# Packing 16 experts into ten blocks of 128 slots instead of eleven, with one more weight buffer

## What is computed

```python
sel = sigmoid(t @ w_router) + router_bias          # 384 tokens, 16 experts in 4 groups
best = argmax(sum of the two largest sel in each group)
idx = top_k(sel inside the best group, 2)          # two experts for each token
gates = one_hot(idx) * scores / sum
hid = silu(t @ w_gate[e]) * (t @ w_up[e])          # 1024 -> 256, for each expert e
out = sum_e (hid * gate_e) @ w_down[e]             # 256 -> 1024
```

## Time and profile before

| | |
|---|---|
| profiled execution | 799.34 us, its span 797.6 us |
| TensorE busy | 742.6 us, 93% |
| VectorE, ACT, POOL busy | 329.5, 216.4, 142.0 us |
| mean granted TensorE clock | 0.989 |
| HBM read and written | 202.02 and 13.93 MB, 271 GB/s over the span |
| layer 0: first gate/up to last down | 262.97 to 396.4 us |
| layer 1: the same | 637.80 to 771.6 us |

### The profile page before, as it was taken

How to read it: one execution, slowest core, us unless ns; L and a number is a source line. 1 busy time by engine, 2 the same in 40 slices (tenths; PEclk the granted TensorE clock), 3 DMA queues, 4 the chain that set the end, 5 groups by cost and what they waited for, 6 DMA issues and landing times. The chain is left out here.

```text
span 797.6 us, 9586 instructions
## 1 busy us (share of the span) xinstructions
PE 742.6 (93%) x3528; PEld 372.2 (47%) x3528; DVE 329.5 (41%) x874; ACT 216.4 (27%) x492; POOL 142.0 (18%) x238
## 2 busy tenths in 40 slices
PE   3999997999999999999999999889999799999994
PEld 1456652455446444443344755345545544444331
DVE  2023534656436453212272262564643734331136
ACT  2210255724023110111312025683312301101121
POOL 4146041120011200000212404222000120000202
PEclk9999998999999999999999999999999999999998
DMA  8997225679422999999897233657420499999961
GB/s 323 387 341 252 95 107 211 219 283 400 181 74 114 390 392 409 424 424 422 315 389 246 83 106 112 212 176 295 190 106 1 158 409 357 418 424 421 424 241 79
DMA packets 66340, 211.56 MB, mean 265 GB/s; under 512 B 7883, under 2 KB 8755, under 8 KB 54003
## 3 DMA queue, kind: packets, MB, share of 16 engines
q1 hardware_dynamic: 52744, 179.33, 58.1%
q10 hardware_dynamic: 7851, 17.70, 5.8%
q0 software_dynamic: 5696, 13.89, 4.9%
HBM read 202.02 MB, written 13.93 MB: 271 GB/s over the span
## 5 line engine op out<-in xcount | busy, mean ns | idle before, releaser
L2228 PE MATMUL bank<-ring,work 128*64 128x512 f32 (+1 forms) x512 | 157.6, 598 | 3.0 <-DMA ring<-in_w_up_dram 2.5
L2228 PEld LDWEIGHTS bank<-ring,work 128*64 128x64 f32 (+1 forms) x512 | 59.1, 158 | 96.0 <-issue 94.4
L2244 PE MATMUL bank<-ring,xs_tok 128*64 128x512 f32 (+1 forms) x256 | 79.9, 597 | 2.0 <-DVE xs_tok L1573 1.0
L1573 DVE COPY xs_tok<-bank 128x256 f32<-128x256 f32 x22 | 9.3, 424 | 149.2 <-PE bank L2235 149.2
L1858 PE MATMUL bank<-hT,ring 128*128 128x384 f32 x192 | 62.2, 486 | 0.0
L1732 PE MATMUL bank<-ring,cpad 128*32 128x512 f32 x384 | 49.4, 636 | 6.6 <-DMA ring<-in_w_ada_dram 5.8
L1858 PEld LDWEIGHTS bank<-hT,ring 128*128 128x128 f32 x192 | 36.5, 190 | 25.0
L2244 PEld LDWEIGHTS bank<-ring,xs_tok 128*64 128x64 f32 (+1 forms) x256 | 28.3, 157 | 39.1 <-issue 35.0
L990 ACT ACTIVATE xs_tok<-bank 128x256 f32<-128x256 f32 x22 | 8.5, 385 | 139.7 <-PE bank L2228 139.7
L2116 PE MATMUL bank<-ring,xn 128*128 128x512 f32 x96 | 43.6, 597 | 0.0
L997 ACT ACTIVATE qkv<-bank 128x512 f32<-128x512 f32 x40 | 21.7, 595 | 79.4 <-PE bank L2244 79.4
(11 more groups left out here) (392 smaller groups left out, 1057.2 us busy)
## 6 DMA issues: line engine op xcount, KB each, us to landing
ring<-in_w_ada_dram SPq DMA_DIRECT2D x48, 1024.0 KB, 8.8
ring<-in_w_gate_dram SPq DMA_DIRECT2D x32, 1024.0 KB, 13.1
ring<-in_w_up_dram SPq DMA_DIRECT2D x32, 1024.0 KB, 16.8
ring<-in_w_down_dram SPq DMA_DIRECT2D x32, 1024.0 KB, 14.6
ring<-in_w_in_dram SPq DMA_DIRECT2D x16, 1024.0 KB, 14.5
ring<-in_w_out_dram SPq DMA_DIRECT2D x8, 1024.0 KB, 7.3
y_exp<-qkv ACTq DMA_DIRECT2D x16, 512.0 KB, 8.4
xpad<-gate_rows ACTq DMA_DIRECT2D x6, 512.0 KB, 4.9
```

The lines of the kernel that those rows point to most:

```text
L1573: dve.tensor_copy(hidT[:, b, :], bank[2][:, 0:F]).then_inc(s_htc, 1)
L2228: last = mm(bank[b][i * n:(i + 1) * n, :].rearrange("p (i f) -> p i f", i=2), rows_T[:, kt * P + i * n:kt * P + (i + 1) * n], gate_up_of(s ...
L2244: last = mm(bank[5 + hf][i * n:(i + 1) * n, :], hidT[:, b, f * P + i * n:f * P + (i + 1) * n], w[:, f, hf * 512:(hf + 1) * 512], start=f = ...
```

## The change

`FIXED` goes from 2 to 3, each fixed expert gets 96 slots, the ranked ones 128 (two), 96 (two), 64 (eight) and 32 (the last). These sum to 1280, ten blocks with no slot left: 0 to 5 hold experts in parts of 32, 64 or 128 slots (an expert may lie in two blocks), 6 to 9 pairs of 64. Blocks 0, 2 and 5 have four parts of 32 columns, each with its own products; block 1 has two of 64. The down unit of pair 1 is loaded in two halves, expert 2's before the ranking. Ahead of it now are experts 0, 1, 2, the down unit of pair 0 and that half. A seventh buffer, `extra`, lies over the normed tiles and padding that the expert stage leaves free, and holds a unit from when the token rows are stored until block 7 at the latest. Each load counts on one of seven semaphores. With the new blocks the planner finds a free slot after nearly every block. `LISTS` becomes 0, 1, 2 to 5, 6 to 9; the list of block 1, which now has expert 2's tokens, is made behind the ranking on VectorE, and on TensorE behind all fillers. A block's result is stored in one or two pieces (twelve in all for seven stored blocks). VectorE's first weighting moves behind the loop.

```diff
-FIXED = 2
+FIXED = 3
-SLOTS = 6
+SLOTS, EXTRA, LANDED = 6, 6, 7
...
-PAIRS = ("fixed", "light", "heavy", "light", "heavy", "light", "light", "light")
...
+FULL, WIDE, NARROW = 2, 4, 12
+FIXED_CAP = 96
+RANK_OF = [None if _x < FIXED else _r for _x, _r in zip(range(E), (0, 0, 0, 2, 0, 1, 3, 12, *range(4, 12)))]
+cap_of = lambda r: CAP if r < FULL else HALF + CAP // 4 if r < WIDE else HALF if r < NARROW else CAP // 4
...
+BLOCKS = [parts_of(*quarters(0, 0, 1, 2), *quarters(1, 0)),
+          parts_of((1, Q, HALF), (2, 0, HALF)),
+          parts_of(*quarters(2, 2), *quarters(3, 0, 1, 2)),
+          parts_of((4, 0, CAP)),
+          parts_of((5, 0, CAP)),
+          parts_of(*quarters(6, 0, 1, 2), *quarters(7, 0))] + [parts_of((x, 0, HALF), (x + 1, 0, HALF)) for x in (8, 10, 12, 14)]
...
+SPLIT = (1, 2)
+MOE_UNITS = [(0, 0), (0, 1), (1, 0), (0, 2), SPLIT]
...
+EXTRA_LAST = STORED
...
+    if in_extra(_u):
+        _holder[EXTRA] = max(_last, default=None)
+    _s = min(_holder, key=lambda s: -1 if _holder[s] is None else RELEASED[_holder[s]])
...
-        xn = sb("xn", NT, DM)
+        arena = sb("arena", NT * DM + XM * 512)
+        xn = arena[:, 0:NT * DM].rearrange("p (t c) -> p t c", t=NT)
...
+        extra = arena[:, DM:DM + UNIT]
...
-        LISTS = ((0, 1), (1, 2), (2, 7), (7, NB))
-        ROWS_AT = 5
+        LISTS = ((0, 1), (1, 2), (2, 6), (6, NB))
+        ROWS_AT = 4
...
+                    if (pair, k) == (SPLIT[0], 1):
                         sp.wait_ge(s_order, l + 1)
...
+                    if EARLIER[u] is not None:
+                        sp.wait_ge(*used(EARLIER[u]))
+                    else:
+                        sp.wait_ge(s_h, 16 * NT * (l + 1))
+                        sp.wait_ge(s_x1, 2 * NT * (l + 1))
...
+                    for x, lo, n, at in stores_of(e):
+                        dma(y_exp[row_at(x) + lo:row_at(x) + lo + n, :], y_buf(e)[at:at + n, :]).then_inc(y_stored[b], 16)
...
-                fixed_one_hot(0)
-                fixed_one_hot(1)
+                one_hots(*LISTS[0])
...
                 slot_tokens(0)
                 step(dve.tensor_reduce(rank.unsqueeze(2), perm_tmp, AX.X, ALU.add))
-                slot_tokens(1)
...
                 dve.tensor_scalar(order, R(4)[:, 16 + FIXED:16 + E], -1.0, float(E), ALU.mult, ALU.add
                                   ).then_inc(s_order, 1)
+                one_hots(*LISTS[1])
                 step(dve.tensor_tensor(by_rank, rt[:, 1, :, FIXED:E].unsqueeze(2).broadcast_to([P, NT, RANKED, RANKED]),
                                        perm.unsqueeze(1).broadcast_to([P, NT, RANKED, RANKED]), ALU.mult))
+                slot_tokens(1)
                 step(dve.tensor_reduce(ranked_pos.unsqueeze(3), by_rank, AX.X, ALU.add))
...
+                    narrow = count_key[:, FIXED:E]
+                    step(dve.tensor_scalar(narrow, rank, float(NARROW), float(Q), ALU.is_gt, ALU.mult))
+                    step(dve.tensor_tensor(cap_row[:, FIXED:E], cap_row[:, FIXED:E], narrow, ALU.subtract))
...
-                    if e == NB - 2:
-                        weighted(0)
+                weighted(0)
                 weighted(1)
...
                 pe.wait_ge(s_btc, 6 * l + 2)
                 clock_kept(4, 2)
                 lists(0)
-                lists(1)
-                clock_kept(4, 4)
+                clock_kept(4, 6)
                 if l == 0:
                     ada_columns(ADA_GAP)
-                clock_kept(4, 4)
+                clock_kept(4, 2)
+                lists(1)
...
-                        for i, s in enumerate(slots):
-                            last = mm(bank[b][i * n:(i + 1) * n, :].rearrange("p (i f) -> p i f", i=2),
-                                      rows_T[:, kt * P + i * n:kt * P + (i + 1) * n], gate_up_of(s)[:, kt, :, :],
+                        for s, at, n in parts:
+                            last = mm(bank[b][at:at + n, :].rearrange("p (i f) -> p i f", i=2),
+                                      rows_T[:, kt * P + at:kt * P + at + n], gate_up_of(s)[:, kt, :, :],
                                       start=kt == 0, stop=kt == KT - 1)
```

More of the change, by code:

```diff
@@ L110, with in_extra @@
 SLOT, EARLIER = [], []
+EXTRA_LAST = STORED
+def in_extra(u):
+    for at in MOE_AT:
+        if at + SLOTS <= u < at + MOE_U:
+            p, k = MOE_UNITS[u - at]
+            return (GU_BLOCK[2 * p + k] <= EXTRA_LAST) if k < 2 else DN_BLOCK[p] < EXTRA_LAST
+    return False
 for _u in range(len(ORDER)):
@@ L469, in columns @@
                     sp.wait_ge(*used(EARLIER[u]))
-                load(u % SLOTS, [(slot(u)[:, 4 * i:4 * i + 4, :], v[:, 4 * i:4 * i + 4, :]) for i in range(2)])
+                load(u % LANDED, [(slot(u)[:, 4 * i:4 * i + 4, :], v[:, 4 * i:4 * i + 4, :]) for i in range(2)])
             def ada_unit(u, n):
@@ L572, in _ @@
             pool.iota(iota[:, CAP + 6:CAP + 6 + E], pattern=[[CAP, E]], base=-1, channel_multiplier=0)
-            at = {r: b * CAP + HALF * i for b, (p, part) in enumerate(BLOCKS) if RANK_AT[p]
-                  for i, r in enumerate(RANK_AT[p][k] for k in part)}
-            for r in range(0, RANKED, 2):
-                pool.iota(iota[:, 192 + r:194 + r], pattern=[[at[r + 1] - at[r], 2]], base=at[r] - 1, channel_multiplier=0)
+            at = ROW_AT[FIXED:]
+            r = 0
+            while r < RANKED:
+                run = next((i for i in range(2, RANKED - r) if at[r + i] - at[r + i - 1] != at[r + 1] - at[r]), RANKED - r)
+                pool.iota(iota[:, 192 + r:192 + r + run], pattern=[[at[r + 1] - at[r] if run > 1 else 0, run]],
+                          base=at[r] - 1, channel_multiplier=0)
+                r += run
             pool.iota(iota[:, 160:160 + E], pattern=[[-1, E]], base=E, channel_multiplier=0).then_inc(s_iota, 1)
@@ L2220, in rows_transposed, with gate_up @@
                     last.then_inc(done, 1)
-                def gate_up(b, rows_T, slots, done, between=None):
-                    n = P // len(slots)
+                def gate_up(b, rows_T, parts, done, between=None):
                     for kt in range(KT):
```

210 lines of the change are left out of this document (119 added, 91 removed).

## The result

The changed kernel takes 796.3 us (median of 20 runs, 787.86 to 799.63), the kernel before 799.92 us (20 runs, 797.27 to 803.07): the ratio is 0.9947, with a 95% interval of 0.9931 to 0.9964. That is 3.6 us faster, and 1.8 us more than the predicted 794.5. The profiled execution is one of the longer ones: 798.94 us, span 797.2, against 799.34 and 797.6 before. A second profile of the same kernel, taken for the experiments, has a span of 794.2.

The account below looks back on a forecast made before the run. The expert stages were taken as balanced, TensorE and the weight stream finishing together, with the stream setting the time from G2 on. Layer 0's -1.0 and layer 1's -3.8 gave -4.8 us: 799.34 to 794.5, range 784 to 802.

Parts of the forecast that it names:

- G2: The end of gate/up of block 2 in a layer's expert stage: 291.2 us in layer 0, 666.8 in layer 1 before.
- (1) Ten blocks: TensorE loses one period, 11.7 us per layer, if nothing else binds; a four-part block costs the same within 0.2 us.
- (2) Earlier units and an earlier order: Before the ranking: 4.5 units instead of 3 are in, and the order of experts is ready about 1 us sooner.
- (3) The stream after G2: Fifteen units stream from G2 on; the last down starts at G2 + 97.0, 4.4 us sooner per layer.
- A clock dip there: At the last gate/up: waiting lowers TensorE's clock, costing 1.0 us, covered by the last down's weights coming 1.1 us later.
- (4) The shift of G2: Block 1's list moved, so its gather gets TensorE on 3.9 us later in layer 0, 1.7 in layer 1.
- no wait before block 1: Sign of a wrong forecast: TensorE not waiting for block 1's rows, where a gap of 3 to 4 us was expected.
- The sentence on the wait for the stored rows: SP's wait for stored rows before the seventh buffer's load is over before it, the first gather being issued at 257.03.
- (5) What is free: Twelve stores on ACT's queue cost nothing; 0.9 us more VectorE work before block 1's hidden product fits its 1.4 us slack.
- (6) The tail: After the last down, results come a block earlier: about 1.1 us saved in layer 1, 0.5 in layer 0.
- The forecast's own case: In both expert stages a late gather shifts G2 and the stream pays: 794.5 us, range 791 to 797, chance 0.43.
- The first rival: Block 1's gather is not late, its list moved into time that costs nothing, G2 stays: 789 us, chance 0.20.

Follow-up runs that it names:

- the run in which both last downs waited for their own weights: Changed kernel with SP's ranked loads waiting for block 0's gathered rows, plus ten fillers before the last gate/up: 789.06 us, ratio 0.9829 to the kernel before.
- the kernel with the repair: Changed kernel, with SP waiting before the first ranked expert's load until block 0's rows are gathered: 786.69 us, ratio 0.9831 to the kernel before.
- twenty fillers: Changed kernel with twenty useless filler products on TensorE before the wait for the last gate/up's weights: 799.95 us, ratio 0.9994 to the kernel before.

## Why the prediction was right, and where it was not

**What bounds the kernel** was right: the weight stream from G2 on. Half a unit less is worth 2.6 us a layer, a unit more behind G2 costs 3.7 (7.5 over two layers), and 4.6 us of added TensorE work a layer cost 1.7, each with an error of 1.5 us a layer.

**(1) Ten blocks.** A four-part gate/up takes 7.05 us, one in two parts 7.09: "the same within 0.2 us" holds. The block taken off did not pay by its 11.7 us; 5 us of it stand as waiting before the last gate/up. The Trainium skill says that a change of tiling mode drains TensorE (TensorEngine Tiling (Array Packing), Key Properties). The trace does not contradict it, but shows no price: from gate/up to gate/up a four-part block takes 11.8 us (291.29 to 303.09 in layer 0), where a period was 11.7 before.

**(2) Earlier units and an earlier order.** The facts were right (1.1 us sooner, 258.05). What they do to the row stores and to the first gather was left out. With the early units ahead of them the row stores of layer 0 landed in a median of 5.4 us (4.4 in the second trace, 2.8 before), and the gather's issue moved from 257.03 to 258.58 or 257.55; the earlier order put the ranked loads ahead of it or 0.6 us behind. So the earlier order was a loss. The early units by themselves are a gain: held back as well, they cost 4.6 us a layer.

**(3) The stream after G2.** G2 + 97.0 was predicted, 96.0 and 97.3 were measured, and 95.2 and 97.0 in the run in which both last downs waited for their own weights. The last gate/up was put at + 83 and came at + 81.4 and + 82.1. The wait before it was put at 8 us and is 5: TensorE comes there at G2 + 76.5 and + 76.9, not + 74.9, and the weights 1 to 1.5 us sooner. A clock dip there was booked at 1.0 us and its cover at 1.1; the dips are 1.7 and 2.4 us, and only in layer 1 of the second trace does the last down still wait for its weights (0.56 us).

**(4) The shift of G2** is the step that failed. It said "all of it shifts G2" of the gather of block 1, +3.9 and +1.7, and took the gather of block 0 as unchanged. In layer 0 the gather of block 0 was late, by 5.2 us (9.2 us from issue to rows, where the kernel before has 4.0) and 1.55 us in its issue, with part of the first transposes and products at the granted 0.50; block 1 then came for nothing, which is one of the prediction's own signs of being wrong ("no wait before block 1"). Together +7.1 (second trace +5.8). In layer 1, where the first gather is 1.4 us ahead of the loads and lands in 4.4 us, it was block 1 as predicted, with 9.95 us of latency (10.3 taken), but with a dip of the clock behind it: +3.2 against 1.7. The sentence on the wait for the stored rows was where it could have been seen: it said that this wait was over before the loads, because the gather used to be issued at 257.03, and did not ask what the added loads do to those stores.
From issue to rows the gathers took 4.0 us with nearly empty queues and 8.5 to 10 beside weight loads. The Trainium skill's fit is 2.0 us plus bytes at 436 GB/s (DMA: Bandwidth & Descriptors, Anatomy of one DMA); for the 70 rows of 4 KB of block 0 that is an estimate of 2.7, short of both.

**(5) What is free** was: neither the stores nor the combination shows as a wait; block 1's hidden product is never waited for. **(6) The tail** is 1.6 us shorter in layer 1, predicted 1.1; layer 0's, predicted 0.5, is not there (+0.2).

**The sum** of -4.8 stands against -3.6 in the medians, and -0.4 and -3.4 in the two traces. Against the first trace G2 was taken 3.2 us too early in layer 0 and 1.5 in layer 1, the stretch behind it 1.1 too long and 0.5 too short, the tails 0.7 too short (layer 0) and 0.5 too long: together 4.3 of the 4.4 us by which that trace is above the sum, the rest is rounding. Against the second it is 1.4, since both stretches behind G2 are 5.3 us shorter there where 4.4 was taken. So the median lies near the forecast because the stream paid somewhat more than its booked 4.4, and the gathers cost 8.5 to 10.3 us where 5.6 were booked. That these two errors have opposite signs is luck: the sum is closer than its terms. The forecast's own case, a gather shifts G2 and the stream pays, is the one that happened, in layer 0 with another gather. The first rival, "the gather is not late", is the kernel with the repair: 786.7, where it said 789.

## What to carry to other kernels

A small transfer that many wait for has to be issued well ahead of large ones (here 1.4 us was enough each time, 1.3 once of two times, 0.6 never), and work that is moved "out of the way" can let the large ones start first: look at which queue gets its order sooner, not only at what the moved step itself delays. Where the engine that waits also releases the next loads, holding the loads back for it can fill the queues better. In the kernel before, whose gather had its lead already, the same wait cost 0.3%. A block taken off an engine pays only what the other resource allows, so ask first what shortens the stream, here the seventh buffer (7.5 us, against a net 3.6 for the whole change).

## What was not expected of the hardware

How much a lead of a microsecond goes with. Gather of block 0, layer 0, from its issue to the transposes of its rows:

| kernel | first ranked load after the gather's issue, us | issue to rows, us |
|---|---|---|
| changed, first trace | -0.53 | 9.2 |
| without the seventh buffer | +0.56 | 8.5 |
| changed, second trace | +0.57 | 8.6 |
| twenty fillers | +1.27 | 7.2 |
| list of block 1 moved back | +1.27 | 4.9 |
| before | +2.14 | 4.0 |
| loads held | +4.86 | 4.0 |

Between 0.57 and 1.43 us of lead the latency falls from 8.6 to 4.4 us (the last pair is layer 1's first gather in the changed kernel). At 1.27 us there are two values. The first load's record in the kernel with twenty fillers is 0.00 us long instead of the usual 0.35, and its second load follows the gather by 1.34 us, against 1.64 with the list moved back (1.02 in the second trace of the changed kernel), so its lead may in truth be the shorter one. What happens in the queues in that time no trace here shows. The other surprise is the clock. The prediction booked 1.0 us for a dip at the last gate/up. After waits of 3.02 to 5.18 us that gate/up, or the one before it, took 8.48 to 9.87 us instead of 7.09, and not in the order of the waits: 8.48 after 4.17 us, 9.85 after 4.20 (the kernels without the seventh buffer and with the early units held). After the waits of 2.96 us and less at that place it took 7.09. Elsewhere shorter waits went either way: with the loads held, the transposes of block 0 in layer 0 took 1.94 us at the granted 0.50 after a wait of 2.01, and with half a unit left out as well 1.06 after 2.02.
